# Channel-major projection, S5 and gated unit, with the S5 scan divided between VectorE and GpSimd

## What is computed

```python
proj = rmsnorm(x, w) @ w_in                       # -> u, z, xbc, dt
bu = einsum('gpc,blgc->blgp', bb, ug)             # S5: 64 groups of 16 channels, 64 complex states each
h = associative_scan(h[t] = a * h[t-1] + bu[t])   # complex, over the tokens, with a start state
y = real(einsum('gcp,blgp->blgc', c, h)) + d * u
g = gelu(y); out = g * sigmoid(g @ w_glu)
y_s5 = rmsnorm(out, s5_norm_w)
x = x + concatenate([y_s5, y_m2]) @ w_out         # y_m2: the Mamba-2 output, gated by silu(z), with a norm
x = x + peer(rmsnorm(x, norm_ffn_w))
```

## Time and profile before

| | |
|---|---|
| median of 3 runs | 4689.3 us (4685.39 to 4689.71) |
| the profiled execution | 4684.25 us, with a span of 4682.5 us |
| PE busy | 2876.1 us (61% of the span) |
| DVE busy | 2462.9 us (53%) |
| ACT busy | 1290.2 us (28%) |
| POOL busy | 1411.9 us (30%) |
| granted TensorE clock, mean | 0.706 of full speed |

### The profile page before, as it was taken

The page is one execution under the profiler, slowest core; times in us unless marked ns, Lnnn a source line. Parts: engine busy times, 40 slices in busy tenths (PEclk is TensorE's granted clock), DMA queues, the critical chain, the costliest instruction groups (busy, mean ns, idle before and its releaser), DMA issues.

```text
span 4682.5 us, 54327 instructions
## 1 busy us (share of the span) xinstructions
PE 2876.1 (61%) x17688; PEld 1481.5 (32%) x17688; DVE 2462.9 (53%) x4924; ACT 1290.2 (28%) x3117; POOL 1411.9 (30%) x1547
## 2 busy tenths in 40 slices
PE   8999590745559995554654744645645546447444
PEld 5766460723334444221311411411312213114110
DVE  1000529248831113576576675674675765766754
ACT  1110020112222321333333333333333333333332
POOL 3000320301100000444444444444443444444443
PEclk9999755866779997665755755756757658658555
DMA  4111300121131112899999999999999999999998
GB/s 163 52 50 36 75 2 2 43 101 30 39 160 66 46 54 97 349 421 420 415 421 400 421 421 405 420 420 404 420 419 400 421 419 405 421 407 420 421 415 362
DMA packets 258478, 1271.27 MB, mean 271 GB/s; under 512 B 63984, under 2 KB 98672, under 8 KB 118128
## 3 DMA queue, kind: packets, MB, share of 16 engines
q0 software_dynamic: 156672, 1140.92, 58.8%
q1 hardware_dynamic: 101536, 127.12, 8.2%
HBM read 1225.69 MB, written 40.09 MB: 270 GB/s over the span
## 4 chain that ended last, share of the span: by engine, by line
DMA 40%; issue 7%; PE 6%; ACT 4%; DVE 4%; POOL 1%; POOLq 0%; SPq 0%; DVEq 0%; ACTq 0%
DMA pe_ring<-in_uv,pe_index_now 39%; PE pe_acc L1858 3%; DVE pe_ring L1781 2%; PE pe_ps_q L1831 2%; ACT pe_mark L1629 1%; ACT pe_weight L1631 1%; PE pe_ps_t L1851 1%; ACT L1629 1%; DVE pe_work_a L1662 1%; POOL pe_ring L1570 1%; ACT L1620 1%; DMA pe_w_q<-in_w_q 0%; DVE pe_pos L1714 0%; DVE pe_work_b L1715 0%; PE pe_ps_s L1841 0%
## 5 line engine op out<-in xcount | busy, mean ns | idle before, releaser
L1781 DVE CUSTOM_DVE_ANT_0 pe_ring<-pe_ring,pe_h_rep 128x1024 f32<-128x1024 f32 x1088 | 1330.7, 1226 | 961.3 <-DMA pe_ring<-in_uv,pe_index_now 881.3
L1858 PE MATMUL pe_acc<-pe_ring,pe_weight 128*32 128x256 f32 x8704 | 1018.5, 560 | 1232.3 <-ACT pe_weight L1631 1203.4
L1570 POOL DMA_INDIRECT pe_ring<-in_uv,pe_index_now x1088 | 1198.0, 1101 | 1471.2 <-PE pe_acc L1858 1275.3
L1858 PEld LDWEIGHTS pe_acc<-pe_ring,pe_weight 128*32 128x32 f32 x8704 | 210.8, 131 | 1973.1 <-ACT pe_weight L1631 1863.6
L1629 ACT ACTIVATE pe_mark<-pe_eye,pe_dot 128x32 f32<-128x32 f32 x1088 | 349.4, 321 | 1744.1 <-DVE pe_dot L1781 1690.3
L1631 ACT ACTIVATE pe_weight<-pe_mark,pe_gate_now 128x32 f32<-128x32 f32 x1088 | 349.5, 321 | 35.1
L1831 PE MATMUL pe_ps_q<-pe_h_t,pe_w_q 128*128 128x128 f32 x2304 | 329.5, 303 | 1.9 <-DMA pe_w_q<-in_w_q 1.9
L1831 PEld LDWEIGHTS pe_ps_q<-pe_h_t,pe_w_q 128*128 128x128 f32 x2304 | 302.7, 213 | 60.1 <-issue 57.8
L372 PE MATMUL pj_bank<-pj_w_in,pj_normed_t 128*128 128x512 f32 (+1 forms) x720 | 267.6, 529 | 5.7 <-DMA pj_w_in<-in_w_in 5.7
L1392 PE MATMUL mo_ps_out<-mo_w_out,mo_both_t 128*128 128x512 f32 x576 | 251.1, 594 | 14.8 <-DVE mo_both_t L1342 11.9
L378 PE MATMUL pj_bank<-pj_normed_t,pj_w_in 128*128 128x128 f32 x1728 | 195.2, 275 | 0.0
(11 more groups left out here) (312 smaller groups left out, 3222.6 us busy)
## 6 DMA issues: line engine op xcount, KB each, us to landing
pe_ring<-in_uv,pe_index_now POOLq DMA_INDIRECT x1088
pe_w_q<-in_w_q SPq DMA_DIRECT2D x4, 2048.0 KB, 18.3
m2s_window<-scratch_xbc SPq DMA_DIRECT2D x8, 786.0 KB
pj_w_in<-in_w_in SPq DMA_DIRECT2D x1, 6144.0 KB, 39.5
scratch_xbc<-pj_chan_out SPq DMA_DIRECT2D x8, 768.0 KB, 5.1
pj_x<-in_x_all SPq DMA_DIRECT2D x9, 512.0 KB
scratch_u<-pj_token_out SPq DMA_DIRECT2D x9, 512.0 KB, 2.6
scratch_z<-pj_token_out SPq DMA_DIRECT2D x9, 512.0 KB, 3.7
```

Of the source, the lines that this page charges most:

```text
L1570: nc.gpsimd.indirect_dma_start(out=ring[:, p, :], out_offset=None, in_=D["uv"], in_offset=bass.IndirectOffsetOnAxis(ap=row, axis=0)).then_ ...
L1781: V.tensor_tensor_reduce(out=ring[:, p, 0:D_MODEL], in0=ring[:, p, 0:D_MODEL], in1=h_rep[:, g % 2, :], scale=1.0, scalar=0.0, op0=ALU.mult ...
L1858: last = T.matmul(acc[j * PER:(j + 1) * PER, g % 2, 0:COLS], lhs(j), src[:, j * COLS:(j + 1) * COLS], start=first, stop=final)
```

## The change

Projection, S5 and gated unit now work with channels on partitions.

- `project_tokens`: the norms and turns of all nine tiles come first and fill `x_t`. Then the products run by pieces of output: 24 pieces of u, 9 of dt, 36 of xbc and 36 of z. For u and xbc the weights are stationary, and a piece has 512, 512 or 80 tokens; for u the moving operand is read in the order of steps within chunks (`"p (k s) -> p s k"`), every eighth float. The weights come in 256-column parts through three buffers. The S5 weights `out_w` and `in_t` are built here, between the pieces, on DVE, PE and ACT.
- `s5_scan`: one block. `u_t` is read from DRAM with 16 DMAs, each of 16 partitions and rows of 552 bytes; no turns on PE are left. After the state products of all pairs, DVE scans pairs 0 to 23 and POOL pairs 24 to 31 (SPLIT=24), POOL after the `b_apart` copies. The output products come after both scans: ten matmuls a pair, eight of them with 64 rows of weights. ACT writes gelu of the result back into `u_t`, from where 32 DMAs of the same shape store `g_t`.
- `mix_out`: first the gated unit for all tokens, in three parts of 368 tokens and eight channel tiles each, with the sum of squares made by a matmul with ones; then the output projection in nine tiles of tokens. z, ym and x have one buffer each.

The names are those of the kernels (digits are left out in rows). Lines with "..." mark what is left out.

```diff
@@ project_tokens: PE @@
-                if j < 5:
-                    a, w = j * 512, 512 if j < 4 else HEADS
-                    for k in range(KT):
-                        last = nc.tensor.matmul(b[:, 0:w], x_t[:, k, :], w_in[:, k, a:a + w],
-                                                start=k == 0, stop=k == KT - 1)
-                else:
-                    for c in range(4):
-                        a = TOKW + ((j - 5) * 4 + c) * P
-                        for k in range(KT):
-                            last = nc.tensor.matmul(b[:, c * P:(c + 1) * P], w_in[:, k, a:a + P],
-                                                    x_t[:, k, :], start=k == 0, stop=k == KT - 1)
+        for i in range(TILES):
+            pe.wait_ge(normed_ready, i + 1)
+            if i:
+                pe.wait_ge(t_copied, i)
+            for k in range(KT):
+                last = T.transpose(t_psum[:, k, :], normed[:, k * P:(k + 1) * P], ident[:])
+            last.then_inc(transposed, 1)
...
+            if e < 3:
+                pe.wait_ge(t_copied, TILES)
+            for k in range(KT):
+                first, final = k == 0, k == KT - 1
+                if kind == "z":
+                    last = T.matmul(b[:, 0:CHUNK], x_t[:, k, part * P:(part + 1) * P], w[:, k, :], start=first, stop=final)
+                elif kind == "d":
+                    last = T.matmul(b[:, 0:HEADS], x_t[:, k, part * P:(part + 1) * P], w_dt[:, k, :], start=first, stop=final)
+                else:
+                    lhs = w[:, k, c % 2 * P:(c % 2 + 1) * P]
+                    toks = x_t[:, k, SEQ:SEQ + REST] if part == 2 else x_t[:, k, part * 512:part * 512 + 512] if kind == "x" else x_t[:, k, 0:SEQ]
+                    if kind == "u":
+                        toks = toks.rearrange("p (k s) -> p s k", s=Q)
+                        toks = toks if part == 2 else toks[:, 4 * part:4 * part + 4, :]
+                    last = T.matmul(source(e, kind, part), lhs, toks, start=first, stop=final)
@@ project_tokens: ACT, and the order of the pieces @@
+        for i in range(TILES):
+            norm(i)
+            if i == 1:
+                act.wait_ge(par_in, 32)
+                A(tmp[:, 0, :], par[:, 2, :], ACT.Exp).then_inc(act_done, 1)
+        act.wait_ge(for_act, 1)
+        A(tmp[:, 3, :], tmp[:, 1, :], ACT.Exp).then_inc(act_done, 1)
...
+pieces = []
+for n, (kind, c) in enumerate(UNITS):
+    if n == U_UNITS:
+        pieces += [(n, "d", 0, t) for t in range(TILES)]
+    if kind == "z":
+        pieces += [(n, "z", c, t) for t in range(TILES)]
+    else:
+        pieces += [(n, kind, 2 * c + half, part) for half in range(2) for part in range(3)]
@@ s5_scan: reading, scan, output @@
-            prompt = state[:, :, :, SEQS:].rearrange("p g h (b j) -> p g h b j", j=SCAN)
-            for j in range(1, SCAN):
-                advance(prompt[:, :, :, :, j], prompt[:, :, :, :, j - 1], 0, BLOCKS)
-            for b in range(1, BLOCKS):
-                advance(prompt[:, :, :, b:b + 1, SCAN - 1], prompt[:, :, :, b - 1:b, SCAN - 1], SCAN - 1, 1)
-            for j in range(SCAN - 1):
-                advance(prompt[:, :, :, 1:, j], prompt[:, :, :, :BLOCKS - 1, SCAN - 1], j, BLOCKS - 1)
...
+    def advance(E, chain, pairs, dst, src, j, n, out=None):
+        count = pairs.stop - pairs.start
+        a, b = t0[:, pairs, :, 0:n], t1[:, pairs, :, 0:n]
+        tab = lambda c: jump[:, j, c, pairs].unsqueeze(2).to_broadcast([P, count, n])
+        for h in range(2):
+            E.tensor_tensor(out=b[:, :, h], in0=src[:, :, 1 - h], in1=tab(2 * h), op=ALU.mult)
+            last = E.tensor_tensor(out=a[:, :, h], in0=src[:, :, h], in1=tab(1), op=ALU.mult)
+        chain.link(last)
+        chain.link(E.tensor_tensor(out=a, in0=a, in1=b, op=ALU.add))
+        chain.link(E.tensor_tensor(out=dst if out is None else out, in0=dst, in1=a, op=ALU.add))
+    def scan_pairs(E, chain, eng, pairs):
+        prompt = state[:, pairs, :, SEQS:].rearrange("p g h (b j) -> p g h b j", j=SCAN)
+        for j in range(1, SCAN):
+            advance(E, chain, pairs, prompt[:, :, :, :, j], prompt[:, :, :, :, j - 1], 0, BLOCKS)
...
+        for j in range(SCAN - 1):
+            advance(E, chain, pairs, prompt[:, :, :, 1:, j], prompt[:, :, :, :BLOCKS - 1, SCAN - 1], j, BLOCKS - 1)
...
+        for n in range(HALVES):
+            for s in range(Q):
+                sp.dma_start(u_t[s * S5_CH:(s + 1) * S5_CH, part(n), :], by_step[s, :, part(n), :]).then_inc(u_in[n], 16)
...
+            groups = slice(2 * n * BATCH, 2 * (n + 1) * BATCH)
+            for s in range(Q):
+                sp.dma_start(out_by_step[s, :, groups, :], u_t[s * S5_CH:(s + 1) * S5_CH, groups, :]).then_inc(g_out, 16)
...
+        chain = Chain(pool, po_step)
+        pool.wait_ge(b_ready, PAIRS // 4)
+        scan_pairs(G, chain, pool, slice(SPLIT, PAIRS))
+        pool.wait_ge(h0_in, 16)
+        G.tensor_copy(rest_start[:, SPLIT:PAIRS, :, SEQS + 1], state[:, SPLIT:PAIRS, :, SEQS]).then_inc(scanned, 1)
...
+        scan_pairs(V, chain, dve, slice(0, SPLIT))
+        dve.wait_ge(h0_in, 16)
+        V.tensor_copy(rest_start[:, 0:SPLIT, :, SEQS + 1], state[:, 0:SPLIT, :, SEQS]).then_inc(scanned, 1)
...
+        for r in range(PAIRS):
+            if r >= 4:
+                pe.wait_ge(y_kept, r - 3)
+            y = [bank[:, 2 * (r % 4) + g, 0:CHUNKS] for g in range(2)]
+            for g in range(2):
+                T.matmul(y[g], toep[:, 2 * r + g, :], u_t[:, 2 * r + g, :], start=True, stop=False)
+            for h in range(2):
+                for g in range(2):
+                    rows = slice(g * 64, g * 64 + 64)
+                    T.matmul(y[g][:, CH_REST:], out_w[rows, r, h, S5_CH:], state[rows, r, h, CH_REST - 1:CHUNKS - 1], start=False, stop=False)
+                for g in range(2):
+                    rows = slice(g * 64, g * 64 + 64)
+                    last = T.matmul(y[g][:, 0:CH_REST], out_w[rows, r, h, S5_CH:], rest_start[rows, r, h, :], start=False, stop=h == 1)
+            last.then_inc(y_made, 1)
@@ mix_out: SP @@
-        with sp.Fori(0, MAIN_TILES) as k:
-            sp.wait_ge(m2_gated, k + 1)
-            sp.wait_ge(g_ready, k + 1)
-            load_y(k + 1)
-            store(k)
-            sp.dma_start(x[:], D["x_all"][bass.ds(k * P + P, P), :]).then_inc(x_in, 16)
+        for c in range(KT):
+            sp.dma_start(g_t[:, c].rearrange("p s k -> p (s k)"), D["g_t"][c * P:(c + 1) * P].rearrange("c s k -> c (s k)")).then_inc(g_in, 16)
+        sp.dma_start(w_glu[:], D["w_glu"]).then_inc(glu_in, 16)
...
+        for k in range(TILES):
+            if k < MAIN_TILES:
+                sp.wait_ge(m2_turned, k + 1)
+                load(k + 1)
+            sp.wait_ge(x_mid_ready, k + 1)
+            sp.dma_start(D["x_mid"][k * P:(k + 1) * P, :], x[:]).then_inc(x_mid_out, 16)
+            if k < MAIN_TILES:
+                sp.wait_ge(x_mid_out, 16 * k + 16)
+                sp.dma_start(x[:], D["x_all"][(k + 1) * P:(k + 2) * P, :]).then_inc(x_in, 16)
@@ mix_out: ACT and DVE @@
+        def gate(k):
+            act.wait_ge(y_in, 32 * k + 32)
+            A(z[:], z[:], ACT.Silu).then_inc(z_ready, 1)
+            act.wait_ge(m2_gated, k + 1)
+            for h in range(2):
+                half = slice(h * 512, h * 512 + 512)
+                last = A(z[:, half], ym[:, half], ACT.Square, accum_out=stat[:, 0, h:h + 1])
+            last.then_inc(m2_summed, 1)
+            act.wait_ge(m2_summed, k + 1)
+            A(stat[:, 1, :], stat[:, 0, :], ACT.Sqrt, bias=eps[:], scale=2.0 / D_MODEL).then_inc(m2_root, 1)
...
+                C = KT * n + c
+                act.wait_ge(glu_made, C + 1)
...
+                A(sig[:, c % 2, :], ps_glu[:, c % 2, 0:N], ACT.Sigmoid).then_inc(sig_ready, 1)
+                act.wait_ge(s5_made, C + 1)
+                if C >= 2:
+                    act.wait_ge(sum_made, C - 1)
+                A(sq[:, c % 2, :], s5_raw[:, c, :], ACT.Square).then_inc(sq_ready, 1)
+            act.wait_ge(sum_made, KT * n + KT)
+            if n:
+                act.wait_ge(s5_ready, KT * n)
+            A(r_b[:], ps_sum[:, 0:N], ACT.Sqrt, bias=eps[:], scale=1.0 / D_MODEL).then_inc(r_root, 1)
...
+        def norm_m2(k):
+            dve.wait_ge(z_ready, k + 1)
+            V.tensor_tensor(out=ym[:], in0=ym[:], in1=z[:], op=ALU.mult).then_inc(m2_gated, 1)
+            dve.wait_ge(m2_root, k + 1)
+            chain.link(V.reciprocal(stat[:, 2, :], stat[:, 1, :]))
+            for h in range(2):
+                half = slice(h * 512, h * 512 + 512)
+                last = V.tensor_scalar(ym[:, half], ym[:, half], stat[:, 2, h:h + 1], None, ALU.mult)
+            last.then_inc(m2_ready, 1)
...
+                V.tensor_tensor(out=by_step(s5_raw[:, c, :]), in0=cut(g_t, c, n), in1=by_step(sig[:, c % 2, :]), op=ALU.mult).then_inc(s5_made, 1)
+            dve.wait_ge(r_root, n + 1)
+            chain.link(V.reciprocal(r_b[:], r_b[:]))
+            for c in range(KT):
```

(49 more changed lines are left out.)

1005 lines of the change are left out of this document (417 added, 588 removed).

## The result

| | before | after |
|---|---|---|
| median | 4688.2 us | 4853.1 us (4852.1 to 4856.1, 4 runs) |
| ratio, 95% interval | | 1.035 (1.034 to 1.037) |
| span of the profiled execution | 4682.5 us | 4851.9 us |
| granted TensorE clock, mean | 0.706 | 0.703 |

The account below looks back on a forecast made before the run. PE bounds projection and mixing, S5 is a chain of short waits; 39 - 171 + 178 = +46 on 4684.25 gives 4730, 4735 as median. Range 4700 to 4775, to 4855 with rival A.

Parts of the forecast that it names:

- Projection: Projection stage: 39 us longer, since nine norms come before the first product; bounds +35 and +50, without the strided read.
- rival A: Projection: PE pays for reading every eighth float in u's products; +78 us at factor 1.7, +112 at 2; chance 0.36.
- u pieces are slow: Projection: sign that the forecast is wrong; u pieces were expected at 7.0 us each, against 12 to 14 if slow.
- The dt pieces: Projection: matmuls of 16 columns priced at 0.232 us each, 17 us in all.
- The first product: Projection: nine norms of 5.05 us each delay PE's first product from 19.0 to 55.5 us.
- S5's load and state products: S5 start: u_t loads at 93 GB/s, second half at +47; state products end at +62 (bounds +40, +70).
- The scans: S5: DVE's and POOL's SBUF multiplies go one after the other; POOL starts at +100, ends last at +200 (bounds +175, +235).
- The output loop: S5: ten matmuls a pair, 48 us if halves overlap, 69 if not; 60 taken plus 2 for the cold clock.
- Mixing: Mixing stage: +178 us; store, loads and gate in series leave PE standing 19 us a tile; stage 618 against 440.
- B: Mixing: the gate's wait is short and the kernel faster; with no wait, 7 x 21 us go, 4590 us; chance 0.08.
- C: S5 shrinks to its low bound: halves overlap, faster load, scans hardly meet; 45 us less, 4690, no change; chance 0.08.

Follow-up runs that it names:

- the reordering: Changed kernel with SP loading z and ym ahead of the store, and DVE making gate and norm ahead of the sum, in mixing's output projection: 4721.9 us.

## Why the prediction was wrong, point by point

- **Projection, the step that failed.** The forecast took nothing for the strided read, because "PE takes 1.7 ns per float32 column, slow enough to hide a second access". It isn't: 3.6 ns a column with every eighth float (14.7 us for 8 x 512). The forecast had this as rival A with 0.36 and as its upper bound a factor 2, 112 us; measured 128, since the factor is 2.1 and the 80-column pieces take 2.35 us (140.55 - 138.20) where 8 x 0.232 = 1.9 was the floor. The row of DVE, which pays, and the Trainium skill's rule of lines stood on one side, and a ratio that no row bore out on the other. (That POOL pays as well was said without a row.) A should have been the forecast. "u pieces are slow" was also the first of its own signs of being wrong, and the only one that came.
- **The dt pieces, a term mis-sized.** 17 us became 29, and 32 with the two turns of `in_w` among them, which slowed with them. They were priced at the earlier trace rows's 0.232 for 16 columns, a matmul between long ones; with nine pieces in a row the clock fell. Where the pieces stand was not in the sum.
- **The first product**: forecast at 55.5, was at 45.0, so 10 us too many. The chain of a norm is 4.15 us in place of 5.05. With only squares and roots on ACT, the table load between them that the earlier trace rows led the forecast to repeat is gone from the fourth norm on, and ACT is no longer what the chain waits for: the root is done at 30.66, but DVE takes it at 32.30, behind the copy that waits for the turn. The chain now goes scale, turn, copy, reciprocal, all between DVE and PE:

```profile
30.37 0.29 ACT L367 ACTIVATE pj_stat<-pj_stat 128x1 f32<-128x1 f32 x1
31.16 1.23 DVE L396 TENSOR_TENSOR pj_x_t<-pj_t_psum,pj_norm_w 128x1024 f32<-128x1024 f32 x1 [2.06 <-PE pj_t_psum L473]
32.30 0.15 DVE L402 RECIPROCAL pj_stat<-pj_stat 128x1 f32<-128x1 f32 x1
```

- **S5's load and state products**: right. Second half at +44 (47), products done at +54 (62). In the load's first 23.5 us the queues moved 109 GB/s, near the 93 of its row.
- **The scans**: the kind was right, the size in part by luck. They end at +193 (200); POOL began at +88 (100) and took 105 us (100). But the working as printed gives +219: wholly in series +232, less 13 for 130 changes of hand at a tenth each; nothing in it leads on to +200. And the two are not simply in series: beside DVE's long multiplies POOL alone pays. What the forecast did not ask is whether the split is worth anything: it loses 20 us against DVE alone.
- **The output loop, a term mis-sized.** 62 us became 98. Its low bound, halves overlapping at 48 us, was right for the array: 98 us at half clock would be about 49 at full, an estimate from the window, and the kernel with one row of start states, which has four short matmuls fewer a pair, took 45. The loop ran at twice its bound since the clock never rose; "2 for the cold clock" assumed that a busy PE gets its full clock.
- **Mixing**: the mechanism as forecast, its size 24 us over. Gap 16.9 (19), tile 47.9 (50.6); seven make 19 of the 24. The store landed in 2.6, not 3.0, ym in 5.7, and the gate took 6.5 in place of 7.8, for its first table load comes early.
- **Rivals.** A came. B did not come for this kernel, but the reordering shows that the wait was not needed, and gave 131 of the 7 x 21 = 147 us named. C did not come: the load and the end of the scans went about as forecast, and the halves did overlap, but at half clock.

The sum, by spans: 46 forecast, +128 strided read, +15 dt, -10 first product, -7 other pieces of projection, -4 its end, +36 output loop, -11 the rest of S5, -24 mixing: 169, as measured. So the terms beside the strided read miss by +51 and -56. That they nearly cancel, and leave the time close to A's, is luck.

What stays open is which mix of columns and rows decides the clock; the runs give four cases (never in 98 us, after some 50 us, and twice within 6 us) and no rule. Open too is what POOL's share would be worth if its scan began with DVE's.

## What to carry to other kernels

Reorder on the copy out of PSUM, not on what PE reads, and ask of each moving operand whether neighbours in it are neighbours in memory. Where a wait stands in a queue ahead of loads that nobody holds up, move the loads before buying buffers. Before giving a second engine a share of a chain of small instructions, look at whether both can read at once, when the second one can begin, and how many instructions, not elements, it gets. And when a row of one engine shows a cost, give the same cost to its neighbour until a row says otherwise.

## What the runs showed of the hardware that was not expected

- PE's moving operand in float32, eight matmuls of 512 columns: 6.9 and 7.2 us at steps of 4 and 8 bytes, 14.4 and 14.7 at 16 and 32.
- In the output loop a PE recorded as busy 97 of 98 us ran all of them at 1.2 GHz. In the projection a PE busy all the time fell from 2.4 GHz within 2 us of the first 16-column matmuls (granted clock 0.94 in the window 299 to 301 us, 0.50 from 301 to 303, after 254 us of long matmuls at 1.00). Matmuls of 10 or 16 columns stood in both places, with the weight load busy for 88 of the 98 us and for all of the 32; leaving them out or spreading them gave the full clock back.
- POOL's multiply of 8 elements took 0.21 us, and 0.62 beside DVE's of 288, which itself took no longer than its size gives (0.66; 0.69 for 312 alone).
